# Delta-rule preparation without GpSimd: masks inside the exponentials' arguments, per-head fused operations, and the first inverse level transposed by TensorE

## The chip, the cores and the metric

The kernel runs on one core of one Trainium2 chip. The metric is device microseconds for one execution of the whole layer. An execution is one launch; inputs lie in HBM, and the host only lays them out. The other seven cores are idle.

Five engines take part: TensorE (PE) multiplies and transposes into PSUM banks, VectorE (DVE) and ScalarE (ACT) work elementwise and can read PSUM, GpSimd (POOL) works elementwise on SBUF, and the queue of SyncE (SP) issues most DMAs. Each engine runs its own list of instructions in order; semaphores tie them together.

## What is computed

One decoder layer on 512 tokens of width 1024. Its token mixer has four differential-attention heads beside four heads of a gated delta rule; its channel mixer is a PEER retrieval over 16384 experts. The change lies in the preparation of the delta rule alone, which the reference writes so (128-wide heads, chunks of C = 64 tokens):

```
incl = tril(ones(C, C)); strict = tril(ones(C, C), k=-1)
gdiff = g[..., :, None] - g[..., None, :]                 # g: cumulated log decay
decay = where(incl, exp(where(incl, gdiff, 0)), 0)
L = where(strict, (beta * k) @ k^T * decay, 0)
sol = triangular_solve(I + L, [beta*v, beta*k*exp(g)])    # unit lower triangle
qk = q @ k^T * decay
```

After it a scan over the 8 chunks carries a 128x128 state per head.

## The kernel before

The layer is one long program. First come the modulation, the input projection and attention; then the delta rule's preparation, which is the stretch of interest (about 248 us to 340 us of the span); then the scan (to about 387 us), the output projection, and from about 457 us the query projection and the two passes over the expert tiles, which fill the rest of the 1809 us.

**Tiles.** The preparation works on NB = 4 blocks t of 128 tokens (two chunks each), with the H = 4 heads side by side, so a tile such as LM[:, t, :] is 128 partitions x 512. The chunks of a block are kept apart by masks of 128x128 that are zero outside the two 64x64 diagonal squares (`masks`; M_STRICT is below the diagonal, M_INCL with the diagonal, M_U above it with the diagonal, MT.. are the blocks of the inverse's levels, transposed, and M_FIRST is the first level untransposed).

**Decay.** TensorE writes in bank ROW_BANK[t] the cumulated decay of each token as rows (L1177, semaphore s_row). For each t VectorE takes four small pieces out of it (L1657, L1660) and writes the difference row - G_CUM into QKT (L1661, s_arg). The difference is then masked twice, into LM with M_INCL and in place with M_U. For t = 0 and 2 GpSimd does this (L573, L575), for t = 1 and 3 VectorE (`masked_args`, L1648, L1650). ScalarE takes the exponential of LM (L806), GpSimd masks the result with M_STRICT (L579, s_mk). ScalarE also takes the exponentials of the rows into egT (L809) and of QKT (L811), which GpSimd masks again later (L590).

**Norms.** q and k are normalised by ScalarE's eight exponentials (L801, s_l2e) and eight VectorE products (L1668, s_l2n), the k heads first. When the four k heads are done, TensorE forms the grams k k^T of the four blocks in banks 4 to 7 (L1186, s_kg).

**L and its inverse.** VectorE multiplies LM by the gram (L1675) and by beta (L1677, s_L). TensorE transposes the result (L1193) and ScalarE copies it to LT (L817). The inverse T of I + L is built in six levels. The first level is I minus the masked L. It is wanted in both orientations: Tm, made by GpSimd from LM (L584, L586, s_t0), and TT, made by VectorE from LT (L1696, L1698, s_td). VectorE then masks LT for the next level back into LM (`masked`, L1692, s_lm).

**Level loop.** Steps n = 0 to 19 (five levels of four blocks) follow. TensorE's order in a step is `level_p(n)` (L1227), `level_t(n-1)` (L1248, L1251), `t_transposes(n-2)` (L1261); at some steps it also forms q k^T (L1202) or transposes v and k (L1211, L1213). ScalarE copies each P (L826) and each transposed T (L830); VectorE subtracts (`updated`, L1713) and masks (L1692). ScalarE's silu of the v heads, one instruction of 128x2048 with a table load, stands ahead of this loop (L819).

The order of work on each engine is written out by hand; nothing is scheduled by a planner. Semaphores count upwards, and a wait names the count. `v.drain()` makes VectorE wait until what it has written is there.

While all this runs, SP's queue writes 24 MB of zeros to HBM for a later stage (until about 296 us); nothing in the preparation waits for it.

## Time and profile before

| what | us |
|---|---|
| runs before (three) | 1811.08, 1811.63, 1811.71; median 1811.63 |
| the profiled execution | 1810.68 |
| its span | 1808.9 |
| decay rows of block 0 ready, VectorE starts on them | 249.3 |
| TensorE starts the grams | 261.8 |
| TensorE starts the inverse's step 0 | 280.3 |
| TensorE starts the inverse's step 3 | 293.4 |
| TensorE starts on u and w, behind the level loop | 339.9 |
| mean granted clock of TensorE | 0.981 |

The time of the profiled execution is its span and 1.8 us around it. In the timelines a row is a start in us, a duration, the engine, the line, the operation, output and inputs, the shapes and how many of them follow one another. A duration covers an instruction from its start to its end, and instructions of one engine overlap a little: with "x2" behind it a row gives the time from the first start to the last end.

### The profile page before, as it was taken

How to read it: one execution, taken by the hardware profiler on the slowest of the kernel's cores; microseconds unless marked ns; L12 is line 12 of the kernel's file. 1: busy time of each engine (PE TensorE's matmuls, PEld its weight loads, DVE VectorE, ACT ScalarE, POOL GpSimd, SP SyncE). 2: the span in 40 equal slices, each digit the busy share in tenths (PEclk: the TensorE clock that was granted, in tenths of full speed). 3: DMA queues.
4: the chain of work that ended last, by engine and by line, in shares of the span. 5: the costliest groups of instructions: out<-in, count | busy, mean ns of one | idle time of the engine just before them, and what ended most of it. 6: DMA issues, size and time to landing. Idle time of an engine off the chain costs nothing.

```text
span 1808.9 us, 25774 instructions
## 1 busy us (share of the span) xinstructions
PE 1698.3 (94%) x7950; PEld 1396.2 (77%) x7950; DVE 1254.7 (69%) x3008; ACT 703.1 (39%) x1036; POOL 938.3 (52%) x748
## 2 busy tenths in 40 slices
PE   4989977996999999999999999999999999999996
PEld 3767757975888888888888888888888887777774
DVE  7677888443216999899899522223788888888885
ACT  4342563533323433433433443443333333333333
POOL 2432335043331057777777777741565666666631
PEclk9999998998999999999999999999999999999998
DMA  7762285014223444444444444466999999999983
GB/s 307 280 232 93 71 338 232 1 36 151 105 82 117 140 146 152 144 145 148 141 151 145 140 149 148 140 232 213 333 335 364 334 364 342 356 353 333 373 311 144
DMA packets 149219, 376.20 MB, mean 208 GB/s; under 512 B 32032, under 2 KB 64928, under 8 KB 145952
## 3 DMA queue, kind: packets, MB, share of 16 engines
q1 hardware_dynamic: 114336, 308.04, 48.1%
q0 software_dynamic: 34816, 67.41, 10.6%
q8 instruction: 24, 0.39, 0.1%
q14 instruction: 43, 0.35, 0.1%
HBM read 312.25 MB, written 63.11 MB: 208 GB/s over the span
## 4 chain that ended last, share of the span: by engine, by line
PE 62%; DVE 15%; DVEq 14%; ACT 6%; issue 2%; POOLq 0%; POOL 0%; ACTq 0%
PE bank L1030 15%; PE bank L1031 15%; PE bank L1032 15%; DVEq L2040 12%; DVE clo L2007 3%; ACT chi L973 3%; DVE coef L2003 3%; DVE ysp L2022 3%; PE bank L1043 2%; PE bank L1044 2%; PE bank L1045 2%; PE bank L1415 1%; PE bank L1419 1%; PE bank L1417 1%; DVE modx L1485 1%
## 5 line engine op out<-in xcount | busy, mean ns | idle before, releaser
L637 POOL DMA_INDIRECT gate_scratch<-merged,idx_cell x384 | 423.5, 1103 | 207.5 <-issue 119.2
L1030 PE MATMUL bank<-act_hi,whi 128*128 128x512 f32 x1312 | 515.1, 393 | 0.1
L1031 PE MATMUL bank<-act_lo,whi 128*128 128x512 f32 x1312 | 511.8, 390 | 0.0
L1032 PE MATMUL bank<-act_hi,wlo 128*128 128x512 f32 x1312 | 511.8, 390 | 0.0
L1866 DVE TENSOR_TENSOR wlo<-raw,whi 128x1024 fp32r<-128x1024 f32 x254 | 309.9, 1220 | 189.4 <-ACT whi L940 186.2
L1415 PE MATMUL bank<-whi,chi 128*128 128x512 f32 x768 | 301.5, 393 | 7.8 <-DVE wlo L1866 7.8
L1419 PE MATMUL bank<-whi,clo 128*128 128x512 f32 x768 | 299.4, 390 | 0.0
L1417 PE MATMUL bank<-wlo,chi 128*128 128x512 f32 x768 | 299.1, 390 | 0.0
L1030 PEld LDWEIGHTS bank<-act_hi,whi 128*128 128x128 f32 x1312 | 247.3, 188 | 51.5 <-DVE act_lo L1509 0.8
L1032 PEld LDWEIGHTS bank<-act_hi,wlo 128*128 128x128 f32 x1312 | 247.0, 188 | 51.7
L1031 PEld LDWEIGHTS bank<-act_lo,whi 128*128 128x128 f32 x1312 | 247.1, 188 | 50.3
L556 POOL TENSOR_TENSOR wlo<-raw,whi 128x1024 fp32r<-128x1024 f32 x52 | 130.8, 2517 | 255.3 <-ACT whi L686 255.3
L655 POOL DMA_INDIRECT rows<-in_expert_tiles,idx_row x128 | 173.7, 1357 | 141.8 <-DVE ysp L2022 118.7
L946 ACT ACTIVATE aout<-bank 128x512 f32<-128x512 f32 x128 | 76.7, 599 | 341.7 <-PE bank L1032 341.4
L973 ACT CAST chi<-coef 128x384 fp32r<-128x384 f32 x128 | 65.6, 513 | 342.6 <-DVE coef L2003 337.9
L646 POOL DMA_INDIRECT asp<-act_scratch,idx_act x128 | 142.3, 1112 | 94.5 <-DMA act_scratch<-aout 55.8
L1415 PEld LDWEIGHTS bank<-whi,chi 128*128 128x128 f32 x768 | 144.1, 188 | 48.7 <-issue 19.9
L2022 DVE SCALAR_TENSOR_TENSOR ysp<-rows,csp,ysp 128x1024 f32<-128x1024 f32 x127 | 163.2, 1285 | 11.8
L1419 PEld LDWEIGHTS bank<-whi,clo 128*128 128x128 f32 x768 | 144.1, 188 | 30.9
L1417 PEld LDWEIGHTS bank<-wlo,chi 128*128 128x128 f32 x768 | 144.3, 188 | 28.0
L940 ACT CAST whi<-raw 128x1024 fp32r<-128x1024 f32 x128 | 133.5, 1043 | 0.3
L987 ACT CAST whi<-raw 128x1024 fp32r<-128x1024 f32 x125 | 130.9, 1047 | 0.0
(309 smaller groups left out, 1901.8 us busy)
## 6 DMA issues: line engine op xcount, KB each, us to landing
raw<-in_expert_tiles SPq DMA_DIRECT2D x256, 512.0 KB, 3.6
act_scratch<-aout SPq DMA_DIRECT2D x128, 256.0 KB, 2.2
gate_scratch<-zeros SPq DMA_DIRECT2D x24, 1024.0 KB, 22.2
a_in<-act_scratch SPq DMA_DIRECT2D x128, 192.0 KB, 6.2
g_in<-gate_scratch SPq DMA_DIRECT2D x128, 192.0 KB, 6.3
modx<-in_mod_tiles SPq DMA_DIRECT2D x32, 512.0 KB, 4.7
raw<-in_in_tiles SPq DMA_DIRECT2D x28, 512.0 KB, 3.7
modr<-in_mod_tiles SPq DMA_DIRECT2D x16, 512.0 KB, 10.1
```

The lines of the kernel that those rows point to most:

```text
L637: g.indirect_dma_start(out=gate_cells, out_offset=bass.IndirectOffsetOnAxis(ap=idx_cell[:, b, k:k + 1], axis=0), in_=merged[:, b, k:k + 1] ...
L646: g.indirect_dma_start(out=asp[:, k:k + 1], out_offset=None, in_=act_cells, in_offset=bass.IndirectOffsetOnAxis(ap=idx_act[:, k:k + 1], ax ...
L655: g.indirect_dma_start(out=rows[:, k % ROWS, :], out_offset=None, in_=expert_rows, in_offset=bass.IndirectOffsetOnAxis(ap=idx_row[:, k:k + ...
L1030: mm(out_bank[:], whi[:, slot, w], act_hi[:, k, :], start=(k == 0), stop=False)
L1031: mm(out_bank[:], whi[:, slot, w], act_lo[:, k, :], start=False, stop=False)
L1032: last = mm(out_bank[:], wlo[:, slot, w], act_hi[:, k, :], start=False, stop=(k == KD - 1))
L1415: mm(o, chi[:, j % WSLOT, a], whi4[:, j % WSLOT, w], start=start, stop=False, skip_group_check=True)
L1417: mm(o, chi[:, j % WSLOT, a], wlo4[:, j % WSLOT, w], start=False, stop=False, skip_group_check=True)
L1419: last = mm(o, clo[:, j % WSLOT, a], whi4[:, j % WSLOT, w], start=False, stop=stop, skip_group_check=True)
L1866: tt(wlo4[:, n % WSLOT, :], raw[:, n % RAW, :], whi4[:, n % WSLOT, :].bitcast(F32), ALU.subtract).then_inc(s_lo, 1)
L2022: stt(out=ysp[:], in0=rows[:, k % ROWS, :], scalar=c, in1=ysp[:], op0=ALU.mult, op1=ALU.add).then_inc(s_axpy, 1)
L2040: v.drain()
```

## The change

- Two masks are made at the start that are added, not multiplied: M_NOT_STRICT is 0 where M_STRICT is 1 and 1e30 elsewhere, M_NOT_U is 0 where M_U is 1 and -1e30 elsewhere. An exponential of such an argument is zero. M_INCL is no longer made.
- VectorE makes both arguments from the rows at once: per block and head one instruction (row - G_CUM) + mask into LM and one into QKT, 8 of 128x128 per block, ahead of the small pieces.
- No mask is applied behind the exponentials. All of GpSimd's operations from the arguments to the second masking of QKT are gone, and so are `masked_args`, s_arg and s_mk.
- L is made by one fused instruction per head, (LM * beta) * gram, in place of two of 128x512. VectorE, not GpSimd, makes Tm from it.
- TT of the first level is no longer computed from LT; TensorE transposes Tm (into banks 4 to 7) and ScalarE copies it.
- VectorE's order is written anew: six of eight norms, then `first_level(t)` with `first_masked(t-1)` and the other two norms between.
- ScalarE takes the exponentials of LM between the fourth and the fifth norm; its silu of v is split into four of 128x512, put into the level loop at steps 1, 2, 4 and 6.

```diff
             for t in range(NB):
-                act.wait_ge(s_du[t % 2], t // 2 + 1)
+                act.wait_ge(s_du[0], t + 1)
                 sc.activation(LM[:, t, :], LM[:, t, :], ACT.Exp, scale=-1.0).then_inc(s_de, 1)
-            act.wait_ge(s_row, NB)
+            for n in range(4, 8):
+                inverse_norm(n)
+            act.wait_ge(s_du[1], NB + 1)
...
                 act.wait_ge(s_LT, t + 1)
                 sc.copy(LT[:, t, :], bank[t][:]).then_inc(s_LTc, 1)
+                act.wait_ge(s_t1, t + 1)
+                sc.copy(TT[:, t, :], bank[4 + t][:]).then_inc(s_td, 1)
             act.wait_ge(s_conv, 12)
-            sc.activation(qkvT[:, 8:12, :], qkvT[:, 8:12, :], ACT.Silu).then_inc(s_silu, 1)
...
                     sc.copy(PM[:, t, :], bank[t % 2][:]).then_inc(s_pc, 1)
+                    if n in V_STEPS:
+                        silu_v(V_STEPS.index(n))
...
                 last.then_inc(s_LT, 1)
+                pe.wait_ge(s_t0, t + 1)
+                for h in range(H):
+                    last = nc.tensor.transpose(bank[4 + t][:, hs(h)], Tm[:, t, hs(h)], ident[:])
+                last.then_inc(s_t1, 1)
...
             for t in range(NB):
                 dve.wait_ge(s_row, t + 1)
                 row = by_head(bank[ROW_BANK[t]][:])
+                for out, m, ready in ((LM, M_NOT_STRICT, s_du[0]), (QKT, M_NOT_U, s_du[1])):
+                    for h in range(H):
+                        last = stt(out=out[:, t, h * HD:(h + 1) * HD], in0=row[:, h, :],
+                                   scalar=g16(G_CUM)[:, 4 * t + h:4 * t + h + 1], in1=masks[:, m, :],
+                                   op0=ALU.subtract, op1=ALU.add)
+                    last.then_inc(ready, 1)
...
-                tt(by_head(QKT[:, t, :]), row, bc(g16(G_CUM), t), ALU.subtract).then_inc(s_arg, 1)
-                if t == 1:
-                    masked_args(1)
...
-                dve.wait_ge(s_mk, t + 1)
-                tt(LM[:, t, :], LM[:, t, :], bank[4 + t][:], ALU.mult)
-                v.drain()
-                tt(by_head(LM[:, t, :]), by_head(LM[:, t, :]), bc(g16(G_BETA), t),
-                   ALU.mult).then_inc(s_L, 1)
+                dve.wait_ge(s_de, t + 1)
+                for h in range(H):
+                    w = slice(h * HD, (h + 1) * HD)
+                    last = stt(out=LM[:, t, w], in0=LM[:, t, w],
+                               scalar=g16(G_BETA)[:, 4 * t + h:4 * t + h + 1], in1=bank[4 + t][:, w],
+                               op0=ALU.mult, op1=ALU.mult)
+                last.then_inc(s_L, 1)
+                v.drain()
+                tt(by_head(Tm[:, t, :]), by_head(LM[:, t, :]), mask4(M_FIRST), ALU.mult)
+                v.drain()
+                tt(by_head(Tm[:, t, :]), ident[:].unsqueeze(1).to_broadcast([P, H, P]),
+                   by_head(Tm[:, t, :]), ALU.subtract).then_inc(s_t0, 1)
...
+            for n in range(6):
+                qk_normed(n)
             for t in range(NB):
-                dve.wait_ge(s_LTc, t + 1)
-                tt(by_head(TT[:, t, :]), by_head(LT[:, t, :]), mask4(MT), ALU.mult)
-                v.drain()
-                tt(by_head(TT[:, t, :]), ident[:].unsqueeze(1).to_broadcast([P, H, P]),
-                   by_head(TT[:, t, :]), ALU.subtract).then_inc(s_td, 1)
-                dve.wait_ge(s_t0, t + 1)
-                masked(t)
+                first_level(t)
+                if t >= 1:
+                    first_masked(t - 1)
+                if t >= 2:
+                    qk_normed(t + 4)
+            first_masked(NB - 1)
```

VectorE at the decay arguments, blocks 0 and 1, before (gsm holds G_CUM and the small pieces; gdn_decay_rows is s_row):

```order
L1657 TENSOR_TENSOR gsm_95<-bank0,gsm_95 64x4 [waits gdn_decay_rows]
L1660 COPY gsm_95<-bank0 128x4
L1657 TENSOR_TENSOR gsm_95<-bank0,gsm_95 64x4
L1660 COPY gsm_95<-bank0 128x4
L1661 TENSOR_TENSOR QKT_105<-bank0,gsm_95 128x512
L1657 TENSOR_TENSOR gsm_95<-bank2,gsm_95 64x4 [waits gdn_decay_rows]
L1660 COPY gsm_95<-bank2 128x4
L1657 TENSOR_TENSOR gsm_95<-bank2,gsm_95 64x4
L1660 COPY gsm_95<-bank2 128x4
L1661 TENSOR_TENSOR QKT_105<-bank2,gsm_95 128x512
L1648 TENSOR_TENSOR LM_104<-QKT_105,masks_90 128x512
L1650 TENSOR_TENSOR QKT_105<-QKT_105,masks_90 128x512
```

and now, block 0 and the head of block 1:

```order
L1646 SCALAR_TENSOR_TENSOR LM_104<-bank0,gsm_95,masks_90 128x128 [waits gdn_decay_rows]
L1646 SCALAR_TENSOR_TENSOR LM_104<-bank0,gsm_95,masks_90 128x128 x3
L1646 SCALAR_TENSOR_TENSOR QKT_105<-bank0,gsm_95,masks_90 128x128 x4
L1652 TENSOR_TENSOR gsm_95<-bank0,gsm_95 64x4
L1655 COPY gsm_95<-bank0 128x4
L1652 TENSOR_TENSOR gsm_95<-bank0,gsm_95 64x4
L1655 COPY gsm_95<-bank0 128x4
L1646 SCALAR_TENSOR_TENSOR LM_104<-bank2,gsm_95,masks_90 128x128 [waits gdn_decay_rows]
```

One difference of 128x512 per block, and two masked products for half of the blocks, became eight instructions of 128x128 for every block.

VectorE between the grams and the level loop, before, from the last block's L on (inv_first_T is GpSimd's s_t0):

```order
L1675 TENSOR_TENSOR LM_104<-LM_104,bank7 128x512 [waits gdn_decays_masked,gdn_grams]
L1677 TENSOR_TENSOR LM_104<-LM_104,gsm_95 128x512
L1696 TENSOR_TENSOR TT_80<-LT_103,masks_90 128x512 [waits gdn_LT_copied]
L1698 TENSOR_TENSOR TT_80<-ident_49,TT_80 128x512
L1692 TENSOR_TENSOR LM_104<-LT_103,masks_90 128x512 [waits inv_first_T]
```

and now, the second and the third block:

```order
L1669 SCALAR_TENSOR_TENSOR LM_104<-LM_104,gsm_95,bank5 128x128 [waits gdn_decay_exp,gdn_grams]
L1669 SCALAR_TENSOR_TENSOR LM_104<-LM_104,gsm_95,bank5 128x128 x3
L1674 TENSOR_TENSOR Tm_79<-LM_104,masks_90 128x512
L1676 TENSOR_TENSOR Tm_79<-ident_49,Tm_79 128x512
L1690 TENSOR_TENSOR LM_104<-LT_103,masks_90 128x512 [waits gdn_LT_copied]
L1669 SCALAR_TENSOR_TENSOR LM_104<-LM_104,gsm_95,bank6 128x128 [waits gdn_decay_exp,gdn_grams]
```

The pair of products for TT became the pair for Tm and moved ahead of the transposition; the mask of the next level (L1692, now L1690) comes one block behind.

TensorE at the same place, before:

```order
L1193 MATMUL bank2<-ident_49,LM_104 128x128 [waits gdn_L]
L1193 MATMUL bank2<-ident_49,LM_104 128x128 x3
L1193 MATMUL bank3<-ident_49,LM_104 128x128 [waits gdn_L]
L1193 MATMUL bank3<-ident_49,LM_104 128x128 x3
L1227 MATMUL bank0<-Tm_79,LM_104 128x128 [waits inv_T_ready,inv_masked]
```

and now:

```order
L1185 MATMUL bank3<-ident_49,LM_104 128x128 [waits gdn_L]
L1185 MATMUL bank3<-ident_49,LM_104 128x128 x3
L1189 MATMUL bank7<-ident_49,Tm_79 128x128 [waits inv_first_T]
L1189 MATMUL bank7<-ident_49,Tm_79 128x128 x3
L1223 MATMUL bank0<-Tm_79,LM_104 128x128 [waits inv_T_ready,inv_masked]
```

Before, step 0 of the inverse stood behind the transposition of the last L alone; now it also stands behind that of the last Tm.

## Rows read from the trace of the kernel before

**Rows 1.** The page: busy time by engine, and the chain that ended last.

```profile
PE 1698.3 (94%) x7950; PEld 1396.2 (77%) x7950; DVE 1254.7 (69%) x3008; ACT 703.1 (39%) x1036; POOL 938.3 (52%) x748
PE 62%; DVE 15%; DVEq 14%; ACT 6%; issue 2%; POOLq 0%; POOL 0%; ACTq 0%
```

**Rows 2.** Timeline of VectorE, 244 to 260 us.

```profile
249.29 0.15 DVE L1657 TENSOR_TENSOR gsm<-bank,gsm 64x4 f32<-64x4 f32 x1 [0.27 <-PE bank L1177]
...
249.88 0.69 DVE L1661 TENSOR_TENSOR QKT<-bank,gsm 128x512 f32<-128x512 f32 x1
```

**Rows 3.** Timeline of VectorE, 276 to 294 us.

```profile
275.13 1.75 DVE L1696 TENSOR_TENSOR TT<-LT,masks 128x512 f32<-128x512 f32 x1
...
280.15 1.75 DVE L1696 TENSOR_TENSOR TT<-LT,masks 128x512 f32<-128x512 f32 x1
...
290.18 0.68 DVE L1696 TENSOR_TENSOR TT<-LT,masks 128x512 f32<-128x512 f32 x1
290.93 0.69 DVE L1698 TENSOR_TENSOR TT<-ident,TT 128x512 f32<-128x512 f32 x1
291.54 0.68 DVE L1692 TENSOR_TENSOR LM<-LT,masks 128x512 f32<-128x512 f32 x1
292.14 0.68 DVE L1713 TENSOR_TENSOR Tm<-Tm,bank 128x512 f32<-128x512 f32 x1
```

**Rows 4.** Timeline of GpSimd, 243 to 300 us.

```profile
281.49 1.53 POOL L586 TENSOR_TENSOR Tm<-ident,Tm 128x512 f32<-128x512 f32 x1
282.98 6.73 POOL L590 TENSOR_TENSOR QKT<-QKT,masks 128x512 f32<-128x512 f32 x4
```

**Rows 5.** VectorE's groups by shape, 60 to 440 us: count, busy us, mean ns.

```profile
L1609 DVE SCALAR_TENSOR_TENSOR pr<-pr,small 128x512 f32<-128x512 f32 x4 | 3.0, 752 | 0.3
...
L1792 DVE SCALAR_TENSOR_TENSOR xs<-bank,small,gate_m 128x512 f32<-128x512 f32 x4 | 2.8, 747 | 0.5 <-issue 0.4
...
L1609 DVE SCALAR_TENSOR_TENSOR pr<-pr,small 128x128 f32<-128x128 f32 x4 | 1.4, 351 | 0.3
```

**Rows 6.** Timeline, 440 to 680 us: two such instructions in a row.

```profile
440.20 1.41 DVE L1792 SCALAR_TENSOR_TENSOR xs<-bank,small,gate_m 128x512 f32<-128x512 f32 x2
```

**Rows 7.** Timeline of TensorE, 243 to 300 us.

```profile
261.82 5.75 PE L1186 MATMUL bank<-qkvT 128*128 128x128 f32 x32 [7.31 <-DVE qkvT L1668]
...
285.29 2.08 PE L1227 MATMUL bank<-Tm,LM 128*128 128x128 f32 x8 [2.93 <-DVE LM L1692]
...
292.88 0.66 PE L1261 MATMUL bank<-ident,Tm 128*128 128x128 f32 x4 [0.52 <-DVE Tm L1713]
293.38 1.06 PE L1227 MATMUL bank<-Tm,LM 128*128 128x128 f32 x8
294.27 1.06 PE L1248 MATMUL bank<-PM,TT 128*128 128x128 f32 x8
```

**Rows 8.** Four stretches: busy us and counts by engine, granted clock, DMA share, GB/s.

```profile
264.00:266.00 2.00, 2.00 (x12) 2.00 (x12) 2.00 (x3) 0.86 (x2) 0.71 (x2) 0.54 1.03 430
272.00:274.00 2.00, 0.98 (x6) 0.74 (x7) 1.93 (x3) 0.59 (x1) 2.00 (x2) 0.67 0.98 406
288.00:290.00 2.00, 1.07 (x6) 0.78 (x4) 2.00 (x2) 0.00 (x0) 1.71 (x2) 0.56 1.02 426
296.00:300.00 4.00, 4.00 (x38) 4.00 (x38) 2.12 (x4) 1.75 (x4) 0.00 (x0) 1.00 0.07 23
```

**Rows 9.** Timeline of ScalarE, 243 to 300 us.

```profile
254.76 4.27 ACT L801 ACTIVATE l2r<-l2r 128x512 f32<-128x512 f32 x8
258.93 1.65 ACT L806 ACTIVATE LM<-LM 128x512 f32<-128x512 f32 x3
...
265.68 2.04 ACT L809 ACTIVATE egT<-bank 128x512 f32<-128x512 f32 x4
...
277.02 1.28 ACT L819 ACT_TABLE_LOAD   x1
278.31 1.91 ACT L819 ACTIVATE qkvT<-qkvT 128x2048 f32<-128x2048 f32 x1
```

More of the change, by code:

```diff
@@ L797, in _, with inverse_norm @@
                               bias=eps_t).then_inc(s_l2r, 1)
-            for n in range(8):
+            def inverse_norm(n):
                 act.wait_ge(s_l2r, n + 1)
@@ L801, in _ @@
                 sc.activation(r, r, ACT.Exp, scale=-0.5).then_inc(s_l2e, 1)
+            for n in range(4):
+                inverse_norm(n)
             for t in range(NB):
-                act.wait_ge(s_du[t % 2], t // 2 + 1)
+                act.wait_ge(s_du[0], t + 1)
                 sc.activation(LM[:, t, :], LM[:, t, :], ACT.Exp, scale=-1.0).then_inc(s_de, 1)
-            act.wait_ge(s_row, NB)
+            for n in range(4, 8):
+                inverse_norm(n)
+            act.wait_ge(s_du[1], NB + 1)
             for t in range(NB):
-                sc.activation(egT[:, t, :], bank[ROW_BANK[t]][:], ACT.Exp)
+                last = sc.activation(egT[:, t, :], bank[ROW_BANK[t]][:], ACT.Exp)
+            last.then_inc(s_de, 1)
             for t in range(NB):
@@ L817, in _, with silu_v @@
                 sc.copy(LT[:, t, :], bank[t][:]).then_inc(s_LTc, 1)
+                act.wait_ge(s_t1, t + 1)
+                sc.copy(TT[:, t, :], bank[4 + t][:]).then_inc(s_td, 1)
             act.wait_ge(s_conv, 12)
-            sc.activation(qkvT[:, 8:12, :], qkvT[:, 8:12, :], ACT.Silu).then_inc(s_silu, 1)
+            def silu_v(h):
+                last = sc.activation(qkvT[:, 8 + h, :], qkvT[:, 8 + h, :], ACT.Silu)
+                if h == H - 1:
+                    last.then_inc(s_silu, 1)
             for k in range(1, 6):
@@ L1456, in _ @@
             v.drain()
-            tt(masks[:, M_INCL, :], ge, same, ALU.mult)
             tt(masks[:, M_U, :], lt, same, ALU.mult)
@@ L1659, in _, with qk_normed @@
                     c = 2 * t + s
-                    v.tensor_copy(g_last[:, 4 * c:4 * c + 4], row[:, :, CH * s + CH - 1])
-                tt(by_head(QKT[:, t, :]), row, bc(g16(G_CUM), t), ALU.subtract).then_inc(s_arg, 1)
-                if t == 1:
-                    masked_args(1)
-            for n in range(8):
+                    last = v.tensor_copy(g_last[:, 4 * c:4 * c + 4], row[:, :, CH * s + CH - 1])
+            last.then_inc(s_du[1], 1)
+            def qk_normed(n):
                 dve.wait_ge(s_l2e, n + 1)
@@ L1692, in masked, with first_masked @@
                 tt(by_head(LM[:, t, :]), by_head(LT[:, t, :]), mask4(MT + 1 + k), ALU.mult).then_inc(s_lm, 1)
[L1694 to L1701 removed]
+            def first_masked(t):
+                dve.wait_ge(s_LTc, t + 1)
+                masked(t)
+            for n in range(6):
+                qk_normed(n)
+            for t in range(NB):
+                first_level(t)
[4 more added lines that the diff above has]
+            first_masked(NB - 1)
             def scaled_vk(t):
```

44 lines of the change are left out of this document (9 added, 35 removed).

## The prediction

> **What bounds the kernel now.** The page first: TensorE is busy in 94% of the span, but the chain that ended last lies on it for only 62%, and for 29% on VectorE and its waits [rows 1]. So there are stretches in which something else sets the end. The clearest for this change is 249 to 293 us. The reader is to see three things there.
>
> First, VectorE never rests: its timeline runs from the first decay row at 249.29 us [rows 2] to the last mask of the first level, which ends its slot at 292.14 us when the first `updated` starts [rows 3], 42.85 us in one queue. TensorE meanwhile waits: 7.31 us ahead of the grams, and again ahead of the inverse's first steps [rows 7]. ScalarE has slack.
>
> Second, much of that queue is waiting in disguise. The three instructions per block of the first level (L1696, L1698, L1692) take 5.02 us from 275.13 to 280.15, and 1.96 us from 290.18 to 292.14 [rows 3]. They are the same instructions on the same shapes. What differs is GpSimd, which works without a pause through the first case and ends its last masks at 289.71 (282.98 + 6.73) [rows 4]. So an instruction of VectorE with two SBUF inputs takes 1.67 us in place of 0.65 while GpSimd works.
>
> Third, from 293.38 us on it is TensorE's turn: 8 passes of 128x128 (a product for four heads) start every 0.89 us (293.38 to 294.27) [rows 7] and it is busy all of 296 to 300 us at full clock [rows 8]. Whatever brings step 3 of the inverse forward shifts all that follows: level loop, scan, projections and expert passes depend on this chain, and no DMA seen here is needed early (the zeros are written by 296 us, where the DMA share falls from 1.0 to 0.07 [rows 8], long before anything asks for them).
>
> **Unit prices.** VectorE, nothing beside it: a two-input product of 128x512 0.61 us from start to start, 0.75 with a drain behind it (291.54 - 290.93, 290.93 - 290.18) [rows 3]. The fused form with a scalar per partition: two of 128x512 last 1.41 us together and one 0.747, so they start 0.66 apart [rows 5, 6]; the overlap is 0.087. For 128x128 no row shows two in a row. One lasts 0.351 [rows 5]; with the same overlap they start 0.264 apart. The ends are 0.264 and, if such short ones don't overlap, 0.351; with the latency that a drain adds, 0.41. I take 0.264, because the row with the same overlap has the same operand kinds (PSUM, scalar, SBUF). In TensorE: a set of 8 passes 0.89 us at full clock, 1.78 at half; four transposes half of that.
>
> **The change part by part, on VectorE's queue.**
>
> 1. Arguments. The four small pieces take 0.59 us per block (249.29 to 249.88) [rows 2] and stay. Eight fused pieces take 8 x 0.264 = 2.11. Four blocks: 4 x 2.70 = 10.8, so this part ends at 249.29 + 10.8 = 260.1. The old form took 0.59 + 0.61 per block, plus two masked pairs of 0.75 + 0.61 for VectorE: 7.5 us if nothing disturbs it. Here the change costs about 3 us.
> 2. Six norms at 0.66, without GpSimd beside them: 260.1 + 4.0 = 264.1. Their exponentials are in time. ScalarE does the first four from 254.76 to 256.9 (0.53 each), then those of LM as the arguments come (the last at 258.6), then the rest [rows 9]. Four k heads are ready at 262.7, and TensorE starts the grams at 262.85, 1 us later than before (261.82). It has been idle and starts at half clock, as before (32 passes in 5.75 us; the clock rose at about 265.9, from 0.54 in 264 to 266) [rows 7, 8]. The first gram stands at 262.85 + 1.78 + 0.1 = 264.7, so VectorE waits 0.6.
> 3. `first_level`, per block: three fused pieces at 0.264, the fourth with drain 0.41, a product with drain 0.75, a product 0.61, together 2.56. With four `first_masked` (0.61) and two norms (0.66) VectorE needs 4 x 2.56 + 4 x 0.61 + 2 x 0.66 = 14.0 and is done at 278.7, against 292.14. The last Tm is ready earlier, since one mask and one norm follow after it (with the last mask): 264.7 + 4 x 2.56 + 2 x 0.61 + 0.66 = 276.8.
> 4. TensorE and ScalarE beside that. Sixteen transposes of Tm and four copies are added. All but the last four lie in TensorE's idle time between two L's. Transposing L and the copies are also in time (per block 4 + 4 transposes and two copies of 0.59 against 2.56 us of VectorE). At the end TensorE transposes the last Tm from 276.95 and then runs P0, P1, T0, P2, T1 and four transposes before P3, which is the instruction at 293.38: 5 x 0.89 + 0.44 = 4.9 us of work at full clock.
> 5. The clock. It fell in 272 to 274 us (0.67) while TensorE did four transposes per block, and rose in 288 to 290 (0.56) [rows 8], about 4.5 us after it took up denser work at 285.29 [rows 7]. In the grams it rose 4.0 us after their start. In the new order work is as sparse up to 276.9, so I expect half clock there. The last transposes take 0.88 (to 277.8). With the rise 4.0 us after 276.95, at 280.95, 3.15 us at half do 1.6 us of the work and 3.3 remain: P3 at 284.3, against 293.38. **Gain 9.1 us.** Bounds: full clock throughout gives 276.95 + 0.44 + 4.9 = 282.3 (gain 11.1), half clock throughout 277.8 + 9.8 = 287.6 (gain 5.8).
> 6. Silu of v. Before, table load and silu (1.28 + 1.91 us) [rows 9] lay in ScalarE's wait. Now the load and a quarter (0.53) stand after the copy of P1, at about 281.9, and end at 283.7. The next copy, P2, is then done at 284.3, and T2 wants it after P3, at 285.2. It hides, with 0.9 us to spare. The other quarters hide in steps of 2.2 us or more, which hold two copies. If the cover were gone, it would cost up to 1.8.
> 7. Nothing. Masks at the start: two products out, two scalar operations in. GpSimd's removed work: it is only waited for.
>
> A rule of the Trainium skill bears on item 6. In these rows the silu starts 1.29 us after its load starts. ScalarE: Activation LUTs, What ACT_TABLE_LOAD costs, puts a switch of tables at 2.66 us, with a drain in it. By that the copy of P2 would be done at 285.7, T2 0.5 us late, and the time 1803.0. The row decides, and no drain shows in it.
>
> **The sum.** The profiled execution took 1810.68, so the same gain gives 1801.6 there. The three runs have a median of 1811.63: 1811.63 - 9.1 = **1802.5**.
>
> **The rivals.**
>
> - *Short fused pieces don't overlap.* There are 48 of them. At 0.351 each they cost 48 x 0.087 = 4.2 more: 1806.7. At 0.41 (44 pieces, 0.146 each) 6.4 more: 1808.9. For it: no row shows two short ones in a row. Against: the overlap of 0.087 in rows 6. The Trainium skill's page VectorE: DVE Perf Modes (The DRAIN you can't avoid; Rules for kernel authors) speaks for this rival: the next operation doesn't start until the pipe is empty, and one should keep the count of operations small and not fuse. Rows 6 (1.41 us for two of 0.747) don't agree with it in full.
> - *The clock is not low, or rises at once.* Gain 11.1: 1800.5. Transposes now come twice as often as when it fell.
> - *The clock stays low until P3.* Gain 5.8: 1805.8.
> - *The clock stays at half in the level loop* (this one ends on the slow side). TensorE is the bound there, and each us at half loses 0.5. The 5.8 that are left at P3 are gone after 11.6 us more at half, that is from about 299 us on; if it held to the end of the loop, some 46 us of work would take 92, and the time would be 1811.6 - 5.8 + 46 = 1852. Against it: from P3 on TensorE has no gaps, and the trace shows the clock rise twice after 4 to 4.5 us of that [rows 7, 8].
> - *The gain is lost behind the preparation,* to a transfer that comes when it comes: within 0.2%. The zeros end at 296 us, the next tiles are asked for by the chain itself. I see nothing for it.
>
> **How the numbers follow.** Forecast 1802.5 (gain 8 to 10.5): 0.65. Pieces without overlap 0.12; clock full at once 0.10; low until P3 0.08; low throughout 0.03; lost behind 0.02. A measurement tells 0.2% (3.6 us) from no change. Faster by more (under 1808.0) are the forecast, both clock cases and most of the first rival: 0.92. Same: the rest of it and the last: 0.05. Slower: 0.03. The range goes from 1 us under the full-clock case, 1799.5, to just above the pieces at 0.351, 1807.0; outside lie 0.03 + 0.02 + some 0.03 of the first rival and a share for what I have not seen.
>
> **What would show it.** In the changed trace: VectorE's first of the six norms at about 260.1 (over 262 says that short pieces don't overlap); grams at 262.9; products with two SBUF inputs at 0.6 to 0.75 us all through 260 to 279; last Tm at 276.8; P3 at 284.3; granted clock 0.5 from about 274 and full from about 281; u and w at 330.8, in place of 339.9, and from there the same distances as before to the end. I am wrong if VectorE's instructions stay at 1.6 us with GpSimd idle, or if TensorE waits in steps 2 to 4 for ScalarE's copies.

## The result

The changed kernel takes 1802.68 us (median of six runs, 1801.06 to 1803.13); the kernel before, with three more runs, 1810.99 us (1810.7 to 1811.71). The ratio is 0.9948, with a 95% interval of 0.9938 to 0.9959: 0.5% faster. Predicted were 1802.5 us, between 1799.5 and 1807.

The profiled execution of the changed kernel took 1801.06 us (span 1799.3). Its page, busy time by engine and the chain:

```profile
PE 1696.9 (94%) x7966; PEld 1395.0 (78%) x7966; DVE 1243.2 (69%) x3040; ACT 705.3 (39%) x1043; POOL 910.0 (51%) x728
PE 62%; DVE 15%; DVEq 13%; ACT 6%; issue 2%; DMA 0%; POOLq 0%; POOL 0%; ACTq 0%
```

As in rows 1, the shares hardly move. GpSimd has 20 instructions and 28 us less. What moved is seen only in the stretch itself. VectorE's timeline, from the first decay row to the first `updated`, answers to rows 2 and 3:

```profile
249.58 1.13 DVE L1646 SCALAR_TENSOR_TENSOR LM<-bank,gsm,masks 128x128 f32<-128x128 f32 x4 [0.27 <-PE bank L1169]
250.63 1.11 DVE L1646 SCALAR_TENSOR_TENSOR QKT<-bank,gsm,masks 128x128 f32<-128x128 f32 x4
...
260.23 3.70 DVE L1661 SCALAR_TENSOR_TENSOR qkvT<-qkvT,l2r 128x512 f32<-128x512 f32 x6
264.89 1.12 DVE L1669 SCALAR_TENSOR_TENSOR LM<-LM,gsm,bank 128x128 f32<-128x128 f32 x4 [0.96 <-PE bank L1178]
...
275.66 0.69 DVE L1674 TENSOR_TENSOR Tm<-LM,masks 128x512 f32<-128x512 f32 x1
276.43 0.69 DVE L1676 TENSOR_TENSOR Tm<-ident,Tm 128x512 f32<-128x512 f32 x1
...
278.24 0.68 DVE L1690 TENSOR_TENSOR LM<-LT,masks 128x512 f32<-128x512 f32 x1
281.68 0.69 DVE L1717 TENSOR_TENSOR Tm<-Tm,bank 128x512 f32<-128x512 f32 x1 [2.75 <-PE bank L1244]
```

Every product lasts 0.68 to 0.69 us, where rows 3 had 1.75 beside GpSimd. The queue is done at 278.9 us, not at 292.1, and VectorE then waits 2.75 us for TensorE, where before it went on without a gap: the bound has changed hands. TensorE, answering to rows 7:

```profile
262.78 5.22 PE L1178 MATMUL bank<-qkvT 128*128 128x128 f32 x32 [7.98 <-DVE qkvT L1661]
...
275.62 1.11 PE L1185 MATMUL bank<-ident,LM 128*128 128x128 f32 x4 [1.12 <-DVE LM L1669]
277.17 1.12 PE L1189 MATMUL bank<-ident,Tm 128*128 128x128 f32 x4 [0.44 <-DVE Tm L1676]
278.08 2.56 PE L1223 MATMUL bank<-Tm,LM 128*128 128x128 f32 x16
280.48 1.16 PE L1244 MATMUL bank<-PM,TT 128*128 128x128 f32 x8
281.47 1.06 PE L1223 MATMUL bank<-Tm,LM 128*128 128x128 f32 x8
282.37 1.06 PE L1244 MATMUL bank<-PM,TT 128*128 128x128 f32 x8
283.26 0.60 PE L1257 MATMUL bank<-ident,Tm 128*128 128x128 f32 x4
283.70 1.06 PE L1223 MATMUL bank<-Tm,LM 128*128 128x128 f32 x8
```

Step 3 of the inverse (P3, the last of these rows) starts at 283.70 us, in place of 293.38. Behind it nothing changes: u and w start at 330.24 (before 339.93), the transposes of x ahead of the query projection at 440.99 (before 451.04).

**How executions are compared below.** The stretch does not begin at the same time in each execution: VectorE's memset of the state, the last instruction ahead of the first decay row, starts anywhere from 248.5 to 250.8 us in the fourteen traces, in kernels whose instructions up to there are the same but for the making of two masks. So a run's effect is read as a distance from that memset. For the kernel before P3 starts 44.85 us behind it (293.38 - 248.53) and u and w 91.40; for the changed kernel 34.87 and 81.41.

| run | median us (before on that chip) | last Tm product | P0 | P0 to P2 | P3 | u and w |
|---|---|---|---|---|---|---|
| before | 1810.99 | | 31.75 | 10.03 | 44.85 | 91.40 |
| changed | 1802.68 (1810.99) | 27.60 | 29.25 | 3.39 | 34.87 | 81.41 |
| again | 1803.76 (1812.0) | 27.60 | 29.25 | 3.50 | 34.97 | 81.52 |
| gpsimd_beside | 1809.14 (1812.0) | 33.56 | 35.21 | 3.97 | 41.40 | 87.95 |
| before_fewer_masks | 1806.79 (1812.0) | | 27.81 | 7.21 | 37.24 | 83.78 |
| tt_on_vector | 1804.87 (1812.0) | 30.35 | 30.45 | 4.66 | 37.33 | 83.88 |
| silu_whole | 1805.12 (1811.74) | 27.60 | 29.25 | 5.58 | 37.05 | 83.61 |
| wide_products | 1804.31 (1811.74) | 28.59 | 30.25 | 4.57 | 37.04 | 83.59 |
| transposes_fourfold | 1802.93 (1811.74) | 29.50 | 30.94 | 2.78 | 35.95 | 82.50 |
| norms_moved | 1802.13 (1811.74) | 25.61 | 27.27 | 4.54 | 34.04 | 80.59 |
| order_and_scalar | 2236.95 (2229.11) | 24.81 | 26.47 | 3.27 | 31.96 | 78.51 |
| order_scalar_warm | 2226.33 (2229.11) | 24.74 | 25.98 | 2.97 | 31.18 | 77.73 |
| order_scalar_warm_2 | 2230.06 (2241.26) | 24.90 | 26.14 | 2.97 | 31.34 | 77.89 |
| warm_only | 2228.03 (2229.11) | 27.60 | 28.84 | 2.78 | 33.84 | 80.40 |

All columns from the third on are starts in us behind the memset, but "P0 to P2", which is the distance between the two and holds P0, P1 and T0: 2.67 us of TensorE's work at full clock (3 x 0.89). The last four runs were disturbed behind the preparation, as told below.

The theory under test: two SBUF inputs make VectorE wait for GpSimd; with GpSimd silent VectorE's queue shrinks, and what is left of the gain depends on TensorE's clock. The rivals: the gain comes from fewer or fused instructions, or from the other order, and GpSimd has nothing to do with it.

### The profile page after: what moved, and what is told of

Its sections match the earlier page's. It is cut to its first block, busy times and chain, and to the rows that moved or that the text cites. A ratio compares the mean times of both kernels' runs of the same rounds, so it can differ in the third digit from the quotient of the medians.

```text
span 1799.3 us, 25812 instructions
## 1 busy us (share of the span) xinstructions
PE 1696.9 (94%) x7966; PEld 1395.0 (78%) x7966; DVE 1243.2 (69%) x3040; ACT 705.3 (39%) x1043; POOL 910.0 (51%) x728
## 4 chain that ended last, share of the span: by engine, by line
PE 62%; DVE 15%; DVEq 13%; ACT 6%; issue 2%; DMA 0%; POOLq 0%; POOL 0%; ACTq 0%
PE bank L1022 15%; PE bank L1023 15%; PE bank L1024 15%; DVEq L2044 12%; DVE clo L2011 3%; ACT chi L965 3%; DVE coef L2007 3%; DVE ysp L2026 3%; PE bank L1035 2%; PE bank L1036 2%; PE bank L1037 2%; DVE modx L1480 1%; PE bank L1411 1%; PE bank L1415 1%; PE bank L1413 1%
```

## The experiments

### again: how much of the spread lies in the preparation

> The changed kernel once more, with nothing altered. Its six times spread over 2.1 us (1801.06 to 1803.13) and the profiled one was the fastest. Theory: the preparation is the same in each execution, so step 3 of the inverse starts at 283.4 to 284.6 us again, and what differs lies in the granted clock of later stretches. Rival: the preparation itself varies, and step 3 is 1 us or more later in a slower execution. Time 1801 to 1803 in both.

P3 came 34.97 us behind the memset, against 34.87, and u and w at 81.52 against 81.41, in an execution whose span was 2.1 us longer (1801.4). So the preparation is the same; 0.85 us of the difference came ahead of it (memset at 249.68 against 248.83) and 1.1 behind the transposes of x. The first expectation holds in its main point. I expected the difference in the granted clock of later stretches; that was not shown, and 0.85 us of it lies earlier. The median, 1803.76 us, is 0.8 above the range expected; the kernel before was 1.0 us slower there too (1812.0 against 1810.99).

### gpsimd_beside: GpSimd put back, but for nothing

```diff
+            pool.wait_ge(s_used, T_OUT)
+            pool.wait_ge(s_kg, 1)
+            for i in range(9):
+                g.tensor_tensor(by_head(wlo[:, 0, 0:512]), masks[:, 0:4, :], masks[:, 4:8, :], ALU.mult)
+                g.drain()
+
             pool.wait_ge(s_kg, 2 * NB)
```

> The changed kernel, with nine products of 128x512 added on GpSimd from the first gram on (264.9 us); they read masks and write a buffer that nothing reads then. No other engine waits for them before 308 us. Contention theory: VectorE's 14 instructions with two SBUF inputs between 265 and 279 us go from 0.69 to about 1.6 us while GpSimd works (15 us), the fused pieces with a PSUM input stay at 1.11 for four; step 3 of the inverse comes about 8 us later (292 in place of 283.7) and the time is about 1811. Rival (the gain came from fewer and reordered instructions, not from GpSimd's absence): no instruction changes, step 3 within 0.5 us, time 1801 to 1803.

Timelines of GpSimd and of VectorE in this run:

```profile
265.27 14.94 POOL L575 TENSOR_TENSOR wlo<-masks 128x512 fp32r<-128x512 f32 x9 [29.73 <-PE bank L1184]
```

```profile
269.89 0.69 DVE L1680 TENSOR_TENSOR Tm<-LM,masks 128x512 f32<-128x512 f32 x1
270.66 1.59 DVE L1682 TENSOR_TENSOR Tm<-ident,Tm 128x512 f32<-128x512 f32 x1
272.18 1.75 DVE L1696 TENSOR_TENSOR LM<-LT,masks 128x512 f32<-128x512 f32 x1
273.85 1.11 DVE L1675 SCALAR_TENSOR_TENSOR LM<-LM,gsm,bank 128x128 f32<-128x128 f32 x4
...
279.01 1.74 DVE L1667 SCALAR_TENSOR_TENSOR qkvT<-qkvT,l2r 128x512 f32<-128x512 f32 x1
...
283.25 0.68 DVE L1696 TENSOR_TENSOR LM<-LT,masks 128x512 f32<-128x512 f32 x1
```

Nobody waits for GpSimd's nine products, and yet the last Tm is 5.96 us later (33.56 against 27.60) and the median is 1809.14 us against 1803.76 for the same kernel without them on the same chip. The mechanism is shown: instructions with two SBUF inputs go from 0.69 to 1.59 to 1.75 us, the fused pieces with a PSUM input stay at 1.11 for four, and behind GpSimd's end (280.2 us) all is as before. The size was less than expected (P3 6.5 us later, not 8; the median 5.4, not 8): the first product behind the fused pieces (L1680, 269.89) does not wait. So not each instruction with two SBUF inputs pays, but each one that follows another of its kind while GpSimd works. Six do so ahead of the last Tm, three at 0.9 us more and three at 1.07 from start to start, which makes 5.9 of the 5.96 us. Why the first is free was not tried.

### before_fewer_masks: the kernel before, with 8 of GpSimd's 20 products left out

```diff
-            for t in range(NB):
-                pool.wait_ge(s_de, t + 1)
-                g.tensor_tensor(by_head(LM[:, t, :]), by_head(LM[:, t, :]), mask4(M_STRICT),
-                                ALU.mult).then_inc(s_mk, 1)
...
-            for t in range(NB):
-                g.tensor_tensor(by_head(QKT[:, t, :]), by_head(QKT[:, t, :]), mask4(M_U),
-                                ALU.mult).then_inc(s_mk, 1)
```

> The kernel before, without GpSimd's masks behind the exponentials (L579 on LM and L590 on QKT are left out, so QKT keeps ones outside its triangle); everything else stays, GpSimd's Tm included. Contention theory: GpSimd is then idle from 283 us on and in 260 to 266, so the first level's three products per block take 1.96 in place of 5.02 us for the last blocks and the norms around 262 to 266 are faster: step 3 of the inverse 4 to 8 us earlier than 293.4, time 1804 to 1808. Rival: VectorE has as many instructions as before, so 1810 to 1812.

LM, too, keeps ones outside its triangle. VectorE has the same instructions in the same order as in the kernel before; only its waits for GpSimd's masks became waits for ScalarE's exponentials, and at none of them did VectorE stand idle in the kernel before. There, with GpSimd at work on its masks of LM, the second masked pair ran so:

```profile
261.85 1.58 DVE L1648 TENSOR_TENSOR LM<-QKT,masks 128x512 f32<-128x512 f32 x1
263.51 1.60 DVE L1650 TENSOR_TENSOR QKT<-QKT,masks 128x512 f32<-128x512 f32 x1
```

In this run the same pair, and then the first level, where GpSimd ends at 281.0 us:

```profile
262.65 0.69 DVE L1640 TENSOR_TENSOR LM<-QKT,masks 128x512 f32<-128x512 f32 x1
263.42 0.69 DVE L1642 TENSOR_TENSOR QKT<-QKT,masks 128x512 f32<-128x512 f32 x1
...
278.08 1.75 DVE L1687 TENSOR_TENSOR TT<-LT,masks 128x512 f32<-128x512 f32 x1
279.91 1.60 DVE L1689 TENSOR_TENSOR TT<-ident,TT 128x512 f32<-128x512 f32 x1
281.43 0.68 DVE L1683 TENSOR_TENSOR LM<-LT,masks 128x512 f32<-128x512 f32 x1
282.03 0.68 DVE L1687 TENSOR_TENSOR TT<-LT,masks 128x512 f32<-128x512 f32 x1
```

P3 is 7.6 us earlier than before (37.24 against 44.85) with VectorE's instructions unchanged, of the 10.0 us that the whole change brings there. The time is 1806.79 us against 1812.0. The rival (fewer instructions) falls. The two runs together put most of the gain on GpSimd's silence: P3 is 6.5 us later when nine products of GpSimd are put beside the changed kernel, and 7.6 earlier when 8 of GpSimd's 20 are taken from the kernel before. They don't add up with the rest to exactly 10.0, since what a wait costs depends on what else bounds that moment.

### tt_on_vector: TT made by VectorE again

```diff
-                act.wait_ge(s_t1, t + 1)
-                sc.copy(TT[:, t, :], bank[4 + t][:]).then_inc(s_td, 1)
...
+                tt(by_head(TT[:, t, :]), by_head(LT[:, t, :]), mask4(MT), ALU.mult)
+                v.drain()
+                tt(by_head(TT[:, t, :]), ident[:].unsqueeze(1).to_broadcast([P, H, P]),
+                   by_head(TT[:, t, :]), ALU.subtract).then_inc(s_td, 1)
                 masked(t)
```

> The changed kernel, but TT of the first level is again made by VectorE from LT (two products per block with a drain) and not by TensorE's transposition of Tm and ScalarE's copy. Theory: VectorE is the only bound up to the last mask, so 4 x (0.75 + 0.61) = 5.4 us are added to its queue. The last TT now stands behind the last LT copy; step 3 comes 4.1 to 5.4 us later, time 1806 to 1808. Rival (TensorE's waits for Tm cost as much as VectorE saves): within 1 us of the changed kernel.

P3 came 2.5 us later, not 4.1 to 5.4, and the median was 1.1 us above that of the changed kernel on the same chip. Both expectations missed, mine by the larger part. TensorE's timeline tells why:

```profile
279.44 1.12 PE L1183 MATMUL bank<-ident,LM 128*128 128x128 f32 x4 [4.04 <-DVE LM L1663]
280.35 3.62 PE L1217 MATMUL bank<-Tm,LM 128*128 128x128 f32 x16
```

And VectorE's, the two pairs for TT that stand ahead of the last L, which comes at 278.27:

```profile
271.15 0.69 DVE L1688 TENSOR_TENSOR TT<-LT,masks 128x512 f32<-128x512 f32 x1
275.70 0.68 DVE L1688 TENSOR_TENSOR TT<-LT,masks 128x512 f32<-128x512 f32 x1
```

P0 now stands behind the transposes of the last L, not of the last Tm. The expectation counted three or four pairs ahead of it; in the order of this kernel they are two (2.7 us, and the last Tm is 2.75 later). L is there one product pair before Tm, and four transposes at half clock (0.9) are not needed: P0 is 1.2 us later (30.45 against 29.25). The rest, 1.3 us, is the pace of P0, P1 and T0 (4.66 in place of 3.39), so the clock. VectorE made the last TT at 284.9, beside steps that TensorE bounds. The transposition by TensorE is worth 1.2 us of chain and 1.3 of clock here, not the 5.4 us of VectorE's time that it frees. The 1.1 us between the medians is no more than the spread of either (1803.58 to 1805.98, and 1803.18 to 1804.91), so the distances carry this reading.

### silu_whole: one silu ahead of the loop

```diff
+            sc.activation(qkvT[:, 8:12, :], qkvT[:, 8:12, :], ACT.Silu).then_inc(s_silu, 1)
...
-                    if n in V_STEPS:
-                        silu_v(V_STEPS.index(n))
```

> The changed kernel with the silu of v whole again (128x2048) ahead of the level loop. ScalarE's last copy of TT ends at 278.9 us; the table load and the silu then hold it to 282.1, while the product P0 is ready at 279.8. Theory (the split hides it): the copy of P0 is 2.3 us late, and TensorE waits that long ahead of T0; step 3 is 2 to 2.5 us later, and the time 1803.5 to 1805.5. Rival (there is slack): within 0.5 us of the changed kernel.

ScalarE and TensorE in this run:

```profile
280.91 1.28 ACT L805 ACT_TABLE_LOAD   x1
282.21 1.91 ACT L805 ACTIVATE qkvT<-qkvT 128x2048 f32<-128x2048 f32 x1
284.02 1.06 ACT L813 COPY PM<-bank 128x512 f32<-128x512 f32 x2
```

```profile
280.06 2.92 PE L1218 MATMUL bank<-Tm,LM 128*128 128x128 f32 x16
284.64 1.16 PE L1239 MATMUL bank<-PM,TT 128*128 128x128 f32 x8 [1.66 <-ACT PM L813]
```

P3 is 2.2 us later, and the median 1805.12 us, 6.6 under the kernel before on that chip, where the changed kernel had 8.3 in its own round. That is the expected 2 to 2.5. The split of the silu is not decoration: before, it lay in a wait that the change itself takes away.

### wide_products: no fused pieces

```diff
-                for out, m, ready in ((LM, M_NOT_STRICT, s_du[0]), (QKT, M_NOT_U, s_du[1])):
-                    for h in range(H):
-                        last = stt(out=out[:, t, h * HD:(h + 1) * HD], in0=row[:, h, :], ...
+                tt(by_head(QKT[:, t, :]), row, bc(g16(G_CUM), t), ALU.subtract)
+                v.drain()
+                tt(by_head(LM[:, t, :]), by_head(QKT[:, t, :]), mask4(M_NOT_STRICT), ALU.add).then_inc(s_du[0], 1)
+                tt(by_head(QKT[:, t, :]), by_head(QKT[:, t, :]), mask4(M_NOT_U), ALU.add).then_inc(s_du[1], 1)
...
+                tt(LM[:, t, :], LM[:, t, :], bank[4 + t][:], ALU.mult)
+                v.drain()
+                tt(by_head(LM[:, t, :]), by_head(LM[:, t, :]), bc(g16(G_BETA), t),
+                   ALU.mult).then_inc(s_L, 1)
```

> The changed kernel with 128x512 products in place of the 48 fused pieces per head: for the arguments a difference, a drain and two sums with masks per block, for L two products with a drain. Worked out from prices seen: 0.75 + 0.61 + 0.61 = 1.97 against 2.08 per block for the arguments, 0.75 + 0.75 = 1.50 against 1.22 for L (with the drain behind each). Sum over four blocks: 0.7 us more. If fusing is what gained: step 3 about 0.7 us later. Rival (instruction count is what costs): 2 us or more earlier. My expectation is within 1 us: fusing is nearly neutral here, time 1801 to 1804.

The last Tm is 1.0 us later (28.59 against 27.60), where 0.7 was worked out: 48 fused pieces of 128x128 are a little cheaper than the 20 products of 128x512 that do the same. The two places differ. For the arguments the wide form is the cheaper one: 12 products for 32 pieces, and the norms begin 0.34 us earlier (11.06 us behind the memset, not 11.40). For L the pieces win: a block takes 1.22 us in four pieces and 1.55 in two products with a drain, 1.3 us over the four blocks. So count does cost something: for L four pieces stand for two products and the drain between them, for the arguments eight stand for three. P3 is 2.2 us later, and the further 1.2 us are again P0, P1 and T0 (4.57 against 3.39). Taken together fusing is nearly neutral on VectorE, and the rival (2 us or more earlier with fewer instructions) falls. Wide arguments with fused L were not tried.

### transposes_fourfold: more work for TensorE where it waits

```diff
-                for h in range(H):
-                    last = nc.tensor.transpose(bank[t][:, hs(h)], LM[:, t, hs(h)], ident[:])
+                for h in range(4 * H):
+                    last = nc.tensor.transpose(bank[t][:, hs(h % H)], LM[:, t, hs(h % H)], ident[:])
                 last.then_inc(s_LT, 1)
```

> The changed kernel with each transposition of L made four times over into the same place (12 more passes of 128x128 per block), so that TensorE is busy in more of 268 to 277 us. Theory (the clock fell for want of work, and half clock costs 1 to 1.5 us before step 3): granted clock stays at 1.0 from 266 us on, step 3 starts 0.5 to 1.3 us earlier than 283.7 less what the extra passes delay the last Tm transposes (nothing if they end before Tm is there), time 0 to 1.3 us less. Rival: the clock falls all the same or the extra passes delay the chain, time equal or more.

Behind the grams the clock did what the theory said. Granted clock in the changed kernel and in this one (the column ahead of the last two):

```profile
278.00:280.00 2.00, 2.00 (x14) 2.00 (x13) 0.92 (x2) 0.75 (x2) 0.00 (x0) 0.66 1.00 414
```

```profile
278.00:280.00 2.00, 1.98 (x18) 1.98 (x19) 1.87 (x3) 0.00 (x0) 0.00 (x0) 1.00 1.01 418
```

P0, P1 and T0 took 2.78 us in place of 3.39. But the first LT was late: VectorE waited 1.8 us for its copy, the last Tm came 1.9 us later, and P3 1.1 us later. Two things made it late, the grams and the first repetitions:

```profile
263.27 6.78 PE L1178 MATMUL bank<-qkvT 128*128 128x128 f32 x32 [7.97 <-DVE qkvT L1661]
269.88 1.91 PE L1185 MATMUL bank<-ident,LM 128*128 128x128 f32 x16
```

The copy of the first LT starts 22.51 us behind the memset, against 19.64 in the changed kernel. Of these 2.9 us the repetitions are 1.3 (1.91 for sixteen transposes, 0.60 for four). The other 1.6 came before any repetition: the grams, the same instructions at the same distance from the memset, took 6.78 us in place of 5.22, since the clock rose at 269.5 us, 6.2 behind their start, and at 265.7 in the changed kernel, 2.9 behind it. So the loss at P3 is not the price of the repetitions alone. They did stand in a place where someone was waiting; warm_only, below, moves them away from there.

### norms_moved: another order on VectorE

```diff
             for t in range(NB):
+                if t == 3:
+                    for n in range(4):
+                        qk_normed(n)
                 dve.wait_ge(s_row, t + 1)
...
-            for n in range(6):
-                qk_normed(n)
             for t in range(NB):
                 first_level(t)
                 if t >= 1:
                     first_masked(t - 1)
-                if t >= 2:
-                    qk_normed(t + 4)
             first_masked(NB - 1)
+            for n in range(4, 8):
+                qk_normed(n)
```

> The changed kernel in another order on VectorE: the four k norms stand ahead of block 3's arguments, and the four q norms behind the last mask of the first level, where VectorE waits 2.75 us for TensorE. Theory (VectorE's queue up to the last Tm is the bound): the grams start at 260.1 in place of 262.8, the wait of 0.96 us for them goes, and 3 norms of 0.61 leave the queue ahead of the last Tm (two ahead of the first level, one inside): last Tm ready 2.8 us earlier, step 3 at about 280.9, time 2.8 us less than the changed kernel, 1798 to 1800. Rival (ScalarE becomes the bound, since the exponentials of the rows come after block 3's arguments and the transposition of L waits for them): 0 to 1 us less.

The last Tm came 2.0 us earlier, not 2.8; P3 only 0.8. Two things took it back. VectorE waited for ScalarE, which had waited for VectorE:

```profile
270.11 0.69 DVE L1693 TENSOR_TENSOR LM<-LT,masks 128x512 f32<-128x512 f32 x1 [0.79 <-ACT LT L800]
```

```profile
262.55 0.63 ACT L786 ACTIVATE LM<-LM 128x512 f32<-128x512 f32 x1 [2.32 <-DVE LM L1655]
```

And the clock rose late. It rose at about 281.4 us (0.64 in 280 to 282), 4.8 us after the last Tm's transposes began at 276.62; in the changed kernel 2.2 us after (279.4, 277.17). P0, P1 and T0 took 4.54 us. The median, 1802.13 us, is above the 1798 to 1800 expected; P3's 0.8 us lies in the rival's range (0 to 1), but the wait for ScalarE makes only 0.8 of the 2.0 us that are missing at P3, and the clock the other 1.2 (4.54 against 3.39).

### order_and_scalar, order_scalar_warm, warm_only: the clock and the order apart

The edit of ScalarE's list (both of the first two), and the repeated transposes (the last two):

```diff
             for t in range(NB):
+                if t == NB - 1:
+                    for n in range(4, 8):
+                        inverse_norm(n)
                 act.wait_ge(s_du[0], t + 1)
...
                 sc.copy(LT[:, t, :], bank[t][:]).then_inc(s_LTc, 1)
+                if t == NB - 1:
+                    sc.activation(QKT[:, t, :], QKT[:, t, :], ACT.Exp)
...
                 sc.copy(TT[:, t, :], bank[4 + t][:]).then_inc(s_td, 1)
+                if t < NB - 1:
+                    sc.activation(QKT[:, t, :], QKT[:, t, :], ACT.Exp)
```

```diff
-                for h in range(H):
-                    last = nc.tensor.transpose(bank[t][:, hs(h)], LM[:, t, hs(h)], ident[:])
+                for h in range(3 * H if t >= 2 else H):
+                    last = nc.tensor.transpose(bank[t][:, hs(h % H)], LM[:, t, hs(h % H)], ident[:])
...
-                for h in range(H):
-                    last = nc.tensor.transpose(bank[4 + t][:, hs(h)], Tm[:, t, hs(h)], ident[:])
+                for h in range(3 * H if t in (1, 2) else H):
+                    last = nc.tensor.transpose(bank[4 + t][:, hs(h % H)], Tm[:, t, hs(h % H)], ident[:])
```

> The order of norms_moved, in which VectorE lost 0.79 us waiting for a copy of ScalarE, with ScalarE's list mended: the q norms' exponentials stand ahead of that of LM's last block (where ScalarE waited 2.3 us), and those of QKT and of the small tiles stand between the copies of LT and TT. Theory (VectorE's queue up to the last Tm is the bound, TensorE's clock behind it): the last Tm product starts 24.9 us after VectorE's memset (norms_moved 25.6, the changed kernel 27.6). Step 3 of the inverse then starts between 31.2 us (clock full at once) and 33.3 us (rise 4.8 us after the last Tm's transposes begin) after the memset, against 34.9 in the changed kernel; time 1799 to 1801.5. Rival (the grams at half clock or ScalarE bind next): last Tm at 25.6 or later.

> As order_and_scalar, with transposes made three times over into the same place where TensorE would idle: Tm of blocks 1 and 2, L of blocks 2 and 3. The first and the last, on which others wait, are single. Theory of the clock: it stays full from the grams' end, P0, P1 and T0 take 2.67 us from start to start as in transposes_fourfold, and step 3 starts 31.2 us after the memset; time 1798.5 to 1800.5, and less spread. Rival: the repetitions delay VectorE, or the clock falls all the same: step 3 at 32.5 us or later.

> The changed kernel with only those repeated transposes. Theory: last Tm as in the changed kernel (product starts 27.6 us after the memset), clock full, P0, P1 and T0 in 2.67 us, step 3 at 33.7 us in place of 34.9: the clock's price in the changed kernel is 1.2 us. Rival: step 3 at 34.9 or later.

> order_scalar_warm once more, with nothing altered. In its first run the kernel before took 2229 us on the same chip, since the expert passes waited for HBM, so its time says nothing; within the preparation step 3 started 31.2 us after the memset in place of 34.9. Theory: where the kernel before takes about 1811 us, the 3.7 us reach the end: 1798 to 1800 against 1802 to 1803.8 of the changed kernel. Rival (later stages give it back, as the distances behind the level loop vary by 1 us): 1801 to 1803.

The times of these four runs can't be used: the kernel before took 2229 us beside three of them and 2241 beside the fourth, on two chips, one of which had given 1811.74 for it in the round of silu_whole. From 557 to 1000 us TensorE was busy for 443 us in the kernel before, in its trace of 1810.68 us, and for 275 in order_scalar_warm_2:

```profile
557.00:1000.00 443.00, 443.00 (x1964) 366.93 (x1963) 414.95 (x1827) 183.49 (x210) 276.71 (x246) 1.00 0.45 145
```

```profile
557.00:1000.00 443.00, 274.77 (x1041) 205.27 (x1039) 237.34 (x1011) 94.49 (x109) 196.81 (x197) 0.75 0.24 76
```

The last expectation puts that down to HBM. The trace does not say so: TensorE and VectorE stood between instructions that waited for nothing that the profile shows ("issue"). Of order_scalar_warm_2, two matmuls that followed each other at 2.8 us:

```profile
702.05 0.59 PE L1025 MATMUL bank<-act_hi,whi 128*128 128x512 f32 x1 [2.21 <-issue]
704.85 0.58 PE L1026 MATMUL bank<-act_lo,whi 128*128 128x512 f32 x1 [2.21 <-issue]
```

What slowed them is open. The preparation lies ahead of that and is undisturbed, and there the distances answered as expected:

- warm_only: the last Tm where it was (27.60), P3 at 33.84 (expected 33.7) against 34.87. Half clock costs the changed kernel 1.0 us ahead of P3. P0, P1 and T0 took 2.78 us, here as in transposes_fourfold, not the 2.67 of the expectations.
- order_and_scalar: last Tm 24.81 (expected 24.9), P3 31.96 (expected 31.2 to 33.3). The clock rose 1.9 us after the last Tm's transposes began.
- order_scalar_warm: P3 31.18, and 31.34 in its second run (expected 31.2). Against the changed kernel 3.5 to 3.7 us less at P3, and the same at u and w (77.7 and 77.9 against 81.4).

TensorE in order_scalar_warm, without a gap:

```profile
272.24 1.53 PE L1192 MATMUL bank<-ident,Tm 128*128 128x128 f32 x12
273.87 1.53 PE L1188 MATMUL bank<-ident,LM 128*128 128x128 f32 x12
275.42 0.66 PE L1192 MATMUL bank<-ident,Tm 128*128 128x128 f32 x4
275.92 1.95 PE L1226 MATMUL bank<-Tm,LM 128*128 128x128 f32 x16
277.90 1.16 PE L1247 MATMUL bank<-PM,TT 128*128 128x128 f32 x8
278.89 1.06 PE L1226 MATMUL bank<-Tm,LM 128*128 128x128 f32 x8
```

That this version is faster from end to end (by 0.2%, if 3.6 us reach the end) is not shown, and the last expectation, on the time, was not put to the test.

## Why the prediction was right, and where it was off

By its own steps, in the profiled execution, whose stretch began 0.3 us later than that of the kernel before:

1. *Bound and disguised waits.* Right. The two GpSimd runs show it from both sides. "VectorE never rests" is not quite so: it waited 1.33 us for the rows of block 1 (250.57 to 251.90). And not every product beside GpSimd takes 1.67 us from start to start, as gpsimd_beside shows.
2. *Unit prices.* The fused piece of 128x128 starts 0.26 us after the one ahead (1.04 to 1.05 for four, 249.58 to 250.63); 0.264 was taken from rows 5 and 6. The rival that short ones don't overlap is out. By the Trainium skill's page VectorE: DVE Perf Modes (Rules for kernel authors) one keeps the count low and doesn't fuse. The runs agree for the arguments (wide_products, with 12 for 32, is 0.34 us faster there) and not for L (8 for 16, 1.3 us slower), and not in sum (1.0 us slower). One price was too high: a norm starts 0.60 us after the one ahead (six in 3.70), not 0.66. It has an immediate, no scalar per partition, and no PSUM input; which of these makes it cheaper was not tried.
3. *Arguments* done at 260.1: measured 260.23, with the 0.3 taken off 259.9. *Grams* at 262.85: 262.78. *First `first_level`* at 264.7: 264.89. *Last Tm* ready at 276.8: 277.1. *VectorE done* at 278.7: 278.9. (The last four are read as they stand, 0.3 included.)
4. *P3* at 284.3: 283.70, so 0.9 us earlier than predicted once the 0.3 are taken off. The step that was off is the clock (item 5). It was to rise at 280.95, 4.0 us after the last transposes begin; it rose at 279.4, 2.2 us after. The bounds of 5.8 and 11.1 us of gain held. The other runs show that 4.0 was a fair middle and that no single value is right: 2.2 and 2.4 us in the changed kernel, 1.9 in order_and_scalar, 2.9 in silu_whole, 3.6 in gpsimd_beside, 4.8 in norms_moved, 4.9 in wide_products, and 5.1 in tt_on_vector (there behind the last L's transposes).
5. *Silu of v* hides: right. ScalarE loaded the table at 281.28, and the copy of P2 was done at 283.7, 0.9 us ahead of T2 (284.59). A switch of tables took 1.30 us from start to start, not the 2.66 that the Trainium skill gives in ScalarE: Activation LUTs (What ACT_TABLE_LOAD costs); the row was the better guide.
6. *The sum.* The stretch gives 10.0 us at P3 from a common start, 0.9 more than the 9.1 that were predicted, and the medians differ by 8.3 (1810.99 - 1802.68), 0.8 less. Most of the 1.7 between the two is the choice of executions: the traced ones differ by 9.6 (1810.68 - 1801.06), the changed kernel's being 1.6 us under its median and that of the kernel before 0.3 under its own. What differs between executions is not the preparation: the stretch begins anywhere within 2.3 us, and the part from the transposes of x to the end took 1357.9 us in the kernel before and 1358.3 and 1359.4 in two executions of the changed one. The forecast also started from 1811.63, the median of three runs, where all six give 1810.99. That the median came out within 0.2 us of the forecast is therefore partly luck: a gain 0.8 us too large (the clock's 0.9 against the 1.7) was taken off a start that was 0.6 too high. Whether the 1.7 us belong to the change or are only spread stays open. In each of the nine undisturbed runs of the table the time gained over the kernel before is less than the gain at P3, by 0.1 to 2.4 us; but all nine lean on the one trace of the kernel before.

The slow rival (half clock in the level loop) did not occur: the clock was 1.00 in each stretch from 280 us to the end of the loop. The gain lost behind the preparation did not occur in the traced executions (9.6 of the 10.0 us reach the end); by the medians a part of 1.7 us is undecided.

## What to carry to other kernels

Look for one instruction with two durations in the same trace, and at who works during the longer one: here a helper engine that "took work off" VectorE made VectorE's own products 2.5 times as long (1.75 us for 0.69). When such a bound falls, list what had hidden in its waits (here a table load and silu, worth 2.2 us) and move it in the same change. Price a new chain of instructions by start-to-start distances of the nearest rows, and give TensorE's clock after a sparse stretch a range, not a value.

## What the runs showed of the hardware

- The time from the start of the last transposes ahead of P0 to full clock was not constant: 1.9 to 5.1 us in eight traces of nearly the same program. P0 to P2 took 3.3 to 4.7 us with it, where no wait for ScalarE came between. At the grams, too, it was 2.9 us in one trace of the changed kernel and 6.2 in transposes_fourfold, whose program is the same up to there. Repeating transposes in TensorE's gaps kept the clock at 1.00 once it had risen in the grams (warm_only, both order_scalar_warm runs, transposes_fourfold), and those three steps took 2.8 to 3.0 us each time.
- Beside GpSimd not each product with two SBUF inputs is slow: in gpsimd_beside the first behind fused pieces with a PSUM input took 0.69 to 0.73 us in the three blocks that GpSimd's work covered, and the next 1.59 to 1.60.
